# Weighting the attention probabilities of the last two prompt units on ScalarE alone

## The reference, cut to what matters

```
s = einsum('bhgtd,bhnd->bhgtn', qg, k) * (NSA_HEAD_DIM ** -0.5) - slopes * dist
p = masked_softmax(s, mask)                  # exp(s - max) / sum
o = g[0] * o_cmp + g[1] * o_slc + g[2] * o_win
```

## Time and profile before

| what | us |
|---|---|
| median of 3 runs | 1824.73 |
| lowest and highest run | 1823.89 and 1827.52 |
| the profiled execution's own time | 1824.67 |
| its span, first to last instruction | 1822.7 |
| PE busy | 1733.7 (95%) |
| DVE, POOL, ACT busy | 1092.1, 831.3, 574.8 |

### The profile page before, as it was taken

How to read it: one execution, slowest core, us unless ns; L and a number is a source line. 1 busy time by engine, 2 the same in 40 slices (tenths; PEclk the granted TensorE clock), 3 DMA queues, 4 the chain that set the end, 5 groups by cost and what they waited for, 6 DMA issues and landing times.

```text
span 1822.7 us, 26098 instructions
## 1 busy us (share of the span) xinstructions
PE 1733.7 (95%) x9958; PEld 1404.4 (77%) x9958; DVE 1092.1 (60%) x2064; ACT 574.8 (32%) x1203; POOL 831.3 (46%) x636
## 2 busy tenths in 40 slices
PE   8999999888999989999989998999999999999997
PEld 7888888764555557767767877888888888888886
DVE  5322210546766555564543038898679768968897
ACT  3311211348887845454541042310110011000202
POOL 3212221324454432222111239985677668666853
PEclk9999999969999979999998999999999999999999
DMA  5011222033000087676654142102011201220105
GB/s 148 24 47 53 73 56 63 24 125 96 7 7 10 10 306 271 217 249 250 207 178 151 43 144 100 47 25 91 24 47 47 70 23 48 68 70 7 41 1 186
DMA packets 89348, 166.51 MB, mean 91 GB/s; under 512 B 21616, under 2 KB 55064, under 8 KB 80968
## 3 DMA queue, kind: packets, MB, share of 16 engines
q1 hardware_dynamic: 78968, 97.73, 16.7%
q0 software_dynamic: 9216, 67.11, 10.1%
q10 hardware_dynamic: 1040, 0.00, 0.0%
HBM read 148.35 MB, written 20.66 MB: 93 GB/s over the span
## 4 chain that ended last, share of the span: by engine, by line
PE 63%; DVE 8%; issue 3%; POOL 2%; ACT 1%; DMA 1%; DVEq 0%; ACTq 0%
PE PS L2906 31%; PE PS L2022 8%; PE PS L312 5%; PE PS L1811 4%; PE PS L1826 4%; PE PS L1839 3%; DVE Z L2966 2%; PE PS L2032 1%; DVE Z L2926 1%; DVE srow L2926 1%; PE PS L2155 1%; PE PS L2040 1%; POOL Z L1670 1%; PE PS L2192 1%; DVE Z L430 1%
## 5 line engine op out<-in xcount | busy, mean ns | idle before, releaser
L2966 DVE TENSOR_TENSOR Z<-PS,Z 128x516 f32<-128x516 f32 x432 | 289.3, 687 | 123.3 <-PE PS L2906 122.4
L2906 PE MATMUL PS<-Z,X 128*128 128x258 f32 x584 | 137.0, 381 | 4.2 <-POOL X L2840 2.6
L2906 PE MATMUL PS<-srow,misc 128*128 128x258 f32 x560 | 133.4, 381 | 0.0
L2022 PE MATMUL PS<-Z 128*128 128x256 f32 x512 | 129.7, 391 | 0.0
L2906 PEld LDWEIGHTS PS<-Z,X 128*128 128x128 f32 x584 | 110.7, 190 | 21.0 <-POOL X L2840 3.0
L1549 POOL DMA_INDIRECT Z<-in_cache_nsa_kv,idx x48 | 49.3, 1026 | 170.0 <-ACT X L2226 100.0
L2906 PEld LDWEIGHTS PS<-srow,misc 128*128 128x128 f32 x560 | 106.2, 190 | 15.6
L1132 DVE TENSOR_TENSOR Z<-PS,Z 128x516 f32<-128x516 f32 x27 | 18.8, 695 | 161.4 <-PE PS L312 161.4
L2906 PE MATMUL PS<-srow,X 128*128 128x258 f32 x480 | 113.3, 380 | 0.0
L2920 ACT ACTIVATE Z<-Z 128x2064 f32<-128x2064 f32 x16 | 30.8, 1924 | 246.7 <-DVE Z L2966 246.7
L2022 PEld LDWEIGHTS PS<-Z 128*128 128x128 f32 x512 | 92.1, 192 | 20.9 <-issue 10.8
(11 more groups left out here) (464 smaller groups left out, 4086.9 us busy)
## 6 DMA issues: line engine op xcount, KB each, us to landing
X<-in_w_ff_down SPq DMA_DIRECT2D x12, 1024.0 KB, 5.4
ring<-in_w_in SPq DMA_DIRECT2D x9, 1024.0 KB, 5.1
X<-in_x_prompt SPq DMA_DIRECT2D x8, 1024.0 KB, 8.4
ring<-in_w_ff_up SPq DMA_DIRECT2D x8, 1024.0 KB, 5.5
Z<-in_w_ff_up SPq DMA_DIRECT2D x8, 1024.0 KB, 5.4
out_y_prompt<-X SPq DMA_DIRECT2D x16, 512.0 KB
Z<-in_w_ff_down SPq DMA_DIRECT2D x4, 1024.0 KB, 4.9
X<-out_y_prompt SPq DMA_DIRECT2D x4, 1024.0 KB, 5.6
```

The lines of the kernel that those rows point to most:

```text
L2022: last = nc.tensor.matmul(product(kind, v), w, x, start=(j == 0), stop=(j == 7))
L2906: last = nc.tensor.matmul(M.PS[:, N_.bank(n, e) + c, 0:HB], x[:, k, c * P:(c + 1) * P], y[:, k, :], start=e in (M1, M2, M5) and k == 0, st ...
L2966: nc.vector.tensor_tensor(N_.part(out, e), N_.view(n, e), N_.part(old, e), ALU.add).then_inc(N_.dve, 1)
```

## The change

```
@@ weighted(n, on_scalar)
         return [(kvh, br, c, w) for kvh in range(KVH) for br, c, w in pieces(n) 
-                if (kvh == 1) == on_scalar]
+                if (kvh == 1 or n >= NSU - 2) == on_scalar]
@@ POOL
-        for m in range(2 * NSU):
+        for m in range(2 * NSU - 4):
             n, g = m // 2, m % 2
             pool.wait_ge(rcr, m + 1)
             for kvh, br, c, w in weighted(n, on_scalar=False):
...
             last.then_inc(normd, 1)
-            if m == 2 * NSU - 3:
-                pool.wait_ge(turned, first_group[NSU - 2])
-                gather_rows(pool, M, A, range(3))
+        pool.wait_ge(turned, first_group[NSU - 2])
+        gather_rows(pool, M, A, range(3))
@@ PE, turn(n, j)
             if j == 0:
-                pe.wait_ge(normd, 2 * n + 2)
+                if n < NSU - 2:
+                    pe.wait_ge(normd, 2 * n + 2)
                 pe.wait_ge(norma, 2 * n + 2)
```

## The result

| | before | after |
|---|---|---|
| median of 20 runs each, us | 1824.83 | 1828.57 |
| lowest and highest | 1820.6 and 1828.34 | 1823.91 and 1834.16 |
| ratio of after to before, 95% interval | | 1.0022 [1.0015, 1.0029] |
| profiled execution's own time | 1824.67 | 1826.06 |

The change makes the kernel slower by 0.22%, some 4.0 us (2.7 to 5.3 by the interval). I had said 1827.4 us, "no change, leaning to slower". The time is in the range; it lies 1.2 us over the point, just at the 0.2% that I had called the limit of what can be told.

The account below looks back on a forecast made before the run. PE work bounds most of the kernel, but PE waits for POOL ahead of unit 15. 1824.67 + 2.42 (ACT's chain) + 0.25 (clock) = 1827.34, with 0.06 for the median 1827.4 us; 8-in-10 range 1824.4 to 1829.3.

Parts of the forecast that it names:

- What bounds: At unit 15's start PE waits for POOL; ACT was done 0.90 us earlier, so only 0.90 us can be won.
- Price of a weighting: On ACT, three more tiles per half move what follows by 0.83 us; four halves add 3.32 us.
- The sum at unit 15: ACT's added 3.32 us less the 0.90 us POOL was later: PE starts unit 15 2.42 us later.
- At unit 14 I had 1.66 us: PE's start of unit 14's transposes moves from 642.18 to 643.84, as ACT ends half 29 later.
- What POOL gives back: POOL loses 12 tiles, so its gathers go out some 2 us earlier, which is worth nothing.
- They move with unit 15: Later gathers and the chain behind 655 us shift with unit 15, so all 2.42 us reach the end.
- The clock: PE's clock may fall ahead of unit 14, slowing its first move: 0 to 0.49 us, taken as 0.25.
- Slower: the clock takes more: Clock falls ahead of unit 14 (0.49 us) and rises later in the cached part (0.7): 1828.4 us, chance 0.16.
- decides from the moment when unit 14's transposes already run at 0.50: Sign for the slower case: PE's granted clock is already at half level during unit 14's transposes.
- Faster: the clock stays up: PE at full clock in unit 15 and up to 668.7, saving 4.6 us: 1822.5 us, chance 0.04.
- the 4.6 us that I put on it: Full-clock saving: 3.0 us on unit 15's turn and products, 1.6 us from 665.34 on.
- It costs nothing: ACT's additions hide or the chain behind 655 us has slack: 1824.7 us, at best 1823.8; chance 0.12.

Follow-up runs that it names:

- dve_share: The changed kernel, with VectorE weighting GpSimd's former share in units 14 and 15 and ScalarE only its own; ratio to before 1.0001 [0.9989, 1.0014].
- warm2_before: The kernel before, with unread small matmuls sized to PE's idle time in units 14, 15 and the first cached steps; ratio to before 1.0000 [0.9988, 1.0012].
- warm2_after: The changed kernel, with unread small matmuls sized to its PE idle time in units 14, 15 and the first cached steps; ratio to before 1.0006 [0.9994, 1.0018].
- unit14_only: Against the kernel before, ScalarE weights both heads in unit 14 alone; GpSimd issues the gathers, then weights its share of unit 15; ratio 1.0014 [1.0000, 1.0027].
- after_again: The changed kernel, unaltered, profiled and timed a second time; ratio to before 1.0023 [1.0010, 1.0035].
- dve_share_filled: The changed kernel, with VectorE taking GpSimd's former share in units 14 and 15, plus small matmuls in PE's idle time; ratios to before 0.9988 and 0.9991.

## Why the prediction came out as it did

**What bounds: right.** ACT was done 0.90 us ahead of POOL, and once POOL was gone it was ACT's end that PE waited for. Every new row says so.

**Price of a weighting, 0.83 us for three tiles, four times: right.** The new rows start at 645.44, 646.27 and 647.09. The sum at unit 15, +2.42 us, measured +2.36 in both traces of the changed kernel and +2.37 with the clock held up. At unit 14 I had 1.66 us; it was 1.59 (1.96 against 0.37).

**What POOL gives back, nothing: right.** dve_share has the same early gathers and the same empty POOL, and it is not slower than before.

**"They move with unit 15. I find nothing behind 655 us that is tied to an earlier time": too simple.** I had expected the cached part 2.4 us later (near 657.9 instead of 655.43); it was 1.81 and 1.39 later behind the zero. In the first trace the clock rose again in unit 15's last products (0.74 in the stretch from 653 to 654, 1.00 from 654), where before it stayed at 0.50. And the cached part's first steps hang on gathers that land, and how long that takes differs from trace to trace. In the chains of before and after the wait is 6.47 us and 7.25 us; in the chains of warm2_before and warm2_after:

```profile
652.68 6.60 DMA srow<-in_cache_nsa_kv,idx
```

```profile
659.29 9.67 DMA Z<-in_cache_nsa_kv,idx
```

The second scores of the first cached sequence come 35.94 us behind the zero before, and 37.20 and 36.66 in the traces of the changed kernel; with filling 34.73 and 36.33. PE's timelines of before and after have them here:

```profile
677.75 1.07 PE L2040 MATMUL PS<-Z,misc 128*32 128x512 f32 x8
```

```profile
676.56 1.07 PE L2040 MATMUL PS<-Z,misc 128*32 128x512 f32 x8
```

Of the 2.36 us 0.7 to 1.6 are left there. The wait for the gathers also swallows part of what an early start could win: warm2_before is 2.3 us earlier at the cached part and 1.2 at the second scores, dve_share 1.8 and 0.4 (the zero's 0.29 taken off), and neither is faster. Each of these is one execution, so the size of this is not settled.

**The clock, 0 to 0.49 us, "I take the middle, 0.25": of the terms of the sum the weakest.** I looked only at unit 14's first move. There it was nothing in both traces of the changed kernel (unit 15 is 2.36 us later, not 2.42 + 0.25); the whole 0.49 showed in unit14_only, at a clock of 0.50. Among the runs of one kernel the time goes with the clock: over 114 runs of the kernel before, the 20 with a mean granted clock up to 0.976 took 1826.7 us on average (mean clock 0.975) and the 31 from 0.980 up 1821.2 (0.9806). That is about 1.0 us for 0.001. The changed kernel has 0.9756 and 0.9762 in its two series, before 0.9782: 0.0026 and 0.0020 less. Were it the same between kernels, that would be 2.6 and 2.0 us. With the chain's 2.4 it is 4.4 to 5.0 us; less the 0.8 to 1.6 that are gone at the second scores it is 2.8 to 4.2, and 4.0 and 4.2 were measured. With the idle time in units 14 and 15 filled, the clock is 0.980 and the cost is down to 0.7 us (interval -1.1 to 2.6).

So it is shown that filling PE's idle time in these two units takes back some 3 us of the changed kernel's time. That it does so by the clock is argued, and two things speak against so simple a sum. The rate doesn't carry over from one kernel to another: warm2_before has 0.0020 more clock than before and the same time. And 0.0020 to 0.0026 of the span are 7 to 9 us more at the lower level (an estimate: 0.001 x 1823 / 0.5 = 3.6 us), which no trace of the changed kernel shows around units 14 and 15.

The Trainium skill (TensorE: Matmul & The Clock Gate, HAM oscillation) describes a kernel of this kind: short bursts of matmuls with waits for data between them, in which the clock falls back in each wait, so that each burst starts at the slow level. Its waits are longer than the ones here. Here the level fell in the 1.90 us of idle time ahead of unit 15; whether idle time costs the changed kernel more than its length in this way, no trace shows.

**Open:** where in the span the additional time at the lower level lies, and with it some 3 of the 4 us, which the traces don't show up to the second scores. The two traces of the changed kernel have 20.5 and 17.1 us of it between 620 and 700 us, and the one of before has 20.5, so they don't show it; they are single executions, and the first was among the quickest. Where no kernel differs from another the same count varies more than that: from 24 to 38 us in the stretch 370 to 440 us, and from 26 to 44 us behind the second scores. The time from the second scores to the end of the span goes from 1144.1 to 1149.8 us over the 14 traces, and the time up to the zero from 639.3 to 643.1.

**The rivals.** "Slower: the clock takes more" came nearest: it gave 3.6 us and 1828.4 (1824.73 + 3.6 is 1828.3), and 4.0 us and 1828.57 were measured. But its mechanism, "decides from the moment when unit 14's transposes already run at 0.50", is not it: in after_again the products of unit 14 ran at half speed and unit 15 was not later. I gave it 0.16, and 0.19 to slower by over 0.2%. That the forecast came within 1.2 us of the median is in part luck: its chain was larger than what is left of it behind the gathers, and its clock term smaller than the rest that the runs show. "Faster: the clock stays up" was wrong beyond its chance: even with the clock of before held at 1.00 to 658 us (warm2_before) the kernel was no faster, so the 4.6 us that I put on it were not there. I had halved all PE time up to 668.7 and forgotten that behind 658 PE waits for gathers anyway. "It costs nothing" is excluded by the interval.

## What to carry to other kernels

When an engine is freed by giving its work to another, first look at how much room the second engine has: here it was done 0.90 us ahead, against 3.32 us of added work, and ACT had no idle time in the stretch although it is busy for only 32% of the span. The engine to give it to was the one that idled there (DVE, 3.35 us ahead of one move in the earlier trace rows), and not the one with the lowest busy share. And follow a delay past the next wait for a transfer: of 2.36 us at unit 15 the traces have 0.7 to 1.6 left at the second scores, while the timed runs lost 4.0. A chain read off one trace gives the place of the cost, and here not its size.

## What was not expected of the hardware

A matmul of constants 128x128 by 128x128 in fp32 took 0.24 us at the full clock (12 in 2.94 us), a transpose of the same form 0.11 in a stream: two records for one and twice the time. And two executions of one unchanged kernel differ by up to 8 us (1820.6 to 1828.34), with the time following the granted clock: the correlation over 114 runs is -0.82. Two profiles of such a kernel can agree in a local place within 0.1 us (9.53 twice at unit 15 in the changed kernel) or differ by 0.5 (6.28 and 6.76 in dve_share_filled), and a single one doesn't give the whole time within 2 us.
